# Differential attention: the turn of the last map put ahead of the values on odd steps

## What is computed

```python
sc = jnp.einsum('bqhmd,bkhmd->bhmqk', qblk, k).astype(jnp.float32) + bias
p = jax.nn.softmax(jnp.where(dist >= 0, sc, NEG), axis=-1)
a = p[:, :, 0] - lam * p[:, :, 1]
return jnp.einsum('bhqk,bkhe->bqhe', a.astype(v.dtype), v)
```

## Time and profile before

| | |
|---|---|
| time, median of 3 runs | 1395.96 us (1395.71 to 1396.17) |
| the profiled execution: its time | 1397.49 us |
| the profiled execution: its span | 1395.7 us |
| PE busy in the span | 1341.1 us, 96% |
| DVE, ACT, POOL busy | 47%, 52%, 55% |
| mean granted clock of PE | 0.993 |
| the 32 steps in the span | from 461.3 to 654.4 us |

### The profile page before, as it was taken

The page is one execution under the profiler, slowest core; times in us unless marked ns, Lnnn a source line. Parts: engine busy times, 40 slices in busy tenths (PEclk is TensorE's granted clock), DMA queues, the critical chain, the costliest instruction groups (busy, mean ns, idle before and its releaser), DMA issues.

```text
span 1395.7 us, 20866 instructions
## 1 busy us (share of the span) xinstructions
PE 1341.1 (96%) x7738; PEld 1098.3 (79%) x7738; DVE 652.4 (47%) x1607; ACT 732.5 (52%) x1549; POOL 767.1 (55%) x770
## 2 busy tenths in 40 slices
PE   6999999999999999999999999999999999999997
PEld 4888777777888787877788888778889887778885
DVE  3223068888251455453420011881463347887135
ACT  4244258888343466656433233892534355887252
POOL 5355255677554465665653534687546534586652
PEclk9999998999999999999999999999999999999999
DMA  6232311100434222220443322425226222002322
GB/s 245 97 120 93 121 61 32 31 29 4 163 105 145 101 76 92 76 103 34 156 176 123 111 98 91 152 92 178 93 84 228 100 91 62 1 16 103 139 91 61
DMA packets 28180, 138.65 MB, mean 99 GB/s; under 512 B 3504, under 2 KB 4016, under 8 KB 16688
## 3 DMA queue, kind: packets, MB, share of 16 engines
q1 hardware_dynamic: 14336, 97.52, 19.8%
q10 hardware_dynamic: 13744, 39.79, 8.3%
HBM read 127.86 MB, written 8.39 MB: 98 GB/s over the span
## 4 chain that ended last, share of the span: by engine, by line
PE 76%; DVE 7%; POOL 7%; ACT 6%; issue 2%; DMA 1%; ACTq 0%; POOLq 0%; SPq 0%; DVEq 0%
PE psum L463 51%; PE psum L497 10%; DVE w_free L1453 2%; PE psum L1400 2%; POOL w_free L1572 2%; PE psum L1353 2%; PE psum L1381 2%; PE psum L1022 2%; ACT w_free L908 2%; POOL w_lo L418 2%; PE psum L996 2%; DVE u_lo L1466 1%; ACT u_hi L1511 1%; PE psum L1366 1%; POOL split L1589 1%
## 5 line engine op out<-in xcount | busy, mean ns | idle before, releaser
L418 POOL TENSOR_TENSOR w_lo<-w_raw,w_hi 128x512 fp32r<-128x512 f32 (+2 forms) x159 | 426.2, 2696 | 327.1 <-ACT w_hi L409 317.8
L409 ACT ACTIVATE w_hi<-w_raw 128x2048 fp32r<-128x2048 f32 (+1 forms) x91 | 169.0, 1857 | 97.8 <-DMA w_raw<-in_weights 82.5
L463 PE MATMUL psum<-w_hi,split 128*128 128x512 f32 x608 | 195.3, 394 | 3.2 <-POOL w_lo L418 2.2
L463 PE MATMUL psum<-u_lo,w_hi 128*128 128x512 f32 (+1 forms) x492 | 194.1, 395 | 0.0
L463 PE MATMUL psum<-u_hi,w_hi 128*128 128x512 f32 (+1 forms) x492 | 191.7, 390 | 0.0
L463 PE MATMUL psum<-u_hi,w_lo 128*128 128x512 f32 (+1 forms) x492 | 191.7, 390 | 0.0
L908 ACT ACTIVATE w_free<-w_free,neg_max 128x512 f32<-128x512 f32 (+3 forms) x256 | 148.4, 585 | 10.1 <-DVE neg_max L1453 9.1
L1466 DVE TENSOR_TENSOR u_lo<-psum,u_hi 128x512 fp32r<-128x512 f32 (+3 forms) x256 | 124.0, 519 | 30.5 <-ACT u_hi L1511 27.9
L463 PEld LDWEIGHTS psum<-w_hi,split 128*128 128x128 f32 x608 | 114.2, 188 | 27.6 <-POOL w_lo L418 3.1
L463 PE MATMUL psum<-w_hi,u_lo 128*128 128x512 f32 (+2 forms) x352 | 133.9, 381 | 1.6 <-DVE u_lo L868 1.2
L463 PE MATMUL psum<-w_lo,u_hi 128*128 128x512 f32 (+2 forms) x352 | 132.4, 376 | 0.0
(11 more groups left out here) (212 smaller groups left out, 2495.4 us busy)
## 6 DMA issues: line engine op xcount, KB each, us to landing
w_raw<-in_weights SPq DMA_DIRECT2D x88, 1024.0 KB, 4.8
x<-x_scratch ACTq DMA_DIRECT2D x12, 512.0 KB, 5.2
gain<-in_gains ACTq DMA_DIRECT2D x10, 512.0 KB, 5.7
gain<-in_strips ACTq DMA_DIRECT2D x16, 256.0 KB, 2.8
spare<-in_strips ACTq DMA_DIRECT2D x16, 256.0 KB, 2.9
x_scratch<-x ACTq DMA_DIRECT2D x8, 512.0 KB, 4.0
gain<-in_near ACTq DMA_DIRECT2D x8, 512.0 KB, 4.3
w_raw<-in_near ACTq DMA_DIRECT2D x8, 512.0 KB, 3.7
```

The source lines that it names most:

```text
L409: high = nc.scalar.activation(w_hi[b][:, c], w_raw[b][:, c], ACT.Copy)
L418: low = nc.gpsimd.tensor_tensor(w_lo[b][:, c], w_raw[b][:, c], w_hi[b][:, c].bitcast(F32), ALU.subtract)
L463: mm = nc.tensor.matmul(dst, lhs, rhs, start=(a == 0 and k == 0 and (wl, ul) == (0, 1)), stop=(a + 1 == u and k + 1 == nk and (wl, ul) == ...
```

## The change

On odd steps from 3 on, `turn(i - 1)` is issued directly behind `scores(i)`, and `values((i - 3) // 2)` behind it. Even steps, and step 1, which have no values, stay as they are. No instruction is added or taken away, and all waits keep their counts.

```diff
             for i in range(f.steps):
                 scores(i)
+                if i >= 1:
+                    turn(i - 1)
                 if i >= 3 and i % 2 == 1:
                     values((i - 3) // 2)
-                if i >= 1:
-                    turn(i - 1)
                 if i >= 5 and i % 2 == 1:
                     turn_heads((i - 5) // 2)
                 if i < f.steps - 4:
```

## The result

Over 7 runs each, the changed kernel takes 1399.6 us (1398.69 to 1401.94), the kernel before 1395.71 (1393.51 to 1396.73). The ratio is 1.0028, with a 95% interval of 1.0018 to 1.0038: slower by 3.9 us, twice what was forecast. The interval lies above 1, and it reaches to both sides of the 0.2% that the prediction took as the limit of what can be told. The profiled execution took 1399.29, span 1397.4, only 1.7 more than the profiled one of before. Why the two differences disagree is the matter of this case.

What follows compares the result with a forecast made beforehand. PE, busy 50.00 of 50.00 us, was taken to bound the 32 steps. Terms 3.1 - 0.4 - 0.7 = +2.0 us on the median 1395.96 gave 1398.0, range 1395.2 to 1401.0.

Steps and rivals of the forecast that it cites:

- Which turns move ahead of their maps: Odd steps: the turn comes before its combined map is done in 3 of 15 swaps, steps 9, 17 and 25.
- The tight ones: Steps 3, 29 and 31: maps ready only 0.24, 0.25 and 0.13 us before the turn is due.
- part 5: Steps 10, 18, 26: POOL's earlier pieces may lie beside `combine`; counted 0, with 0.1 to 0.3 us each if it runs over.
- The rival of more waits: Steps 3, 11, 19, 27, 29 and 31 run over by 0.1 us each: +2.5 us in all; chance 0.07.
- part 1: Steps 9, 17, 25: PE waits 1.03 us each, 3.1 in all, from 1.74 shortened by earlier exponentials and POOL pieces.
- In its strict form: Shared-port lock as full block: `combine(8)` needs its whole 0.35 us behind POOL's end, 0.2 more per wait; +2.6, chance 0.06.
- part 2: Step 31: PE's one wait for the last combined map goes, 0.4 us gained, bounds 0.26 and 0.7.
- part 3: PE in 15 odd steps: a cheaper seam from transpose to value product, 0.05 us each, 0.7 gained.
- part 4: Odd steps: values move 0.1 to 0.4 us later; costs nothing, as head squares come after the exponentials; nothing gained.
- The sum: Whole kernel: 3.1 for waits, less 0.4 for the last turn and 0.7 for seams, gives +2.0 us.
- one fall on top of the forecast: Clock rival: behind the three waits PE's granted clock falls once, costing 1.7 us: +3.7, 1399.7 us; chance 0.14.
- the clock falls behind them: Sign that the prediction is wrong: the granted clock falls behind the waits of steps 9, 17 and 25.

Runs made afterwards that it cites:

- the second set of runs: The changed kernel itself measured once more against the kernel before, with a second trace: 1400.86 us (5 runs), ratio 1.0037.
- the two runs that move POOL's pieces: Against the changed kernel: units of steps 7, 15, 23 split one step later (1393.92 us), or only POOL's second two pieces of each one step later (1394.18 us).
- two chunks ahead: Against the changed kernel: in steps 9, 17 and 25 two chunks of fill (six products) between scores and turn; 1395.23 us, ratio 0.9994.
- the run without the three steps: Against the changed kernel: steps 9, 17 and 25 back to the old order, twelve swaps stay; 1394.61 us, ratio 0.9996.

## Why the prediction was right, and where it fell short

- **Which turns move ahead of their maps.** Three of 15, in steps 9, 17 and 25, as forecast. The tight ones held: in steps 3, 29 and 31 PE lost nothing. `combine(10)` did fall beside POOL's pieces (1.61 us in the trace of the changed kernel), as part 5 feared, and so did `combine(18)` and `combine(26)`. They ended 0.4, 0.2 and 0.4 ahead of their turns, where the kernel before had over 1.5 to spare. The rival of more waits, which gave them 0.1 to 0.3, was near.
- **The size of the wait (part 1).** Forecast 1.03, measured 1.02 (0.97 by the step, which holds the seam too, and 0.95 in the list of waits). Both halves of the argument were tested: without the other twelve swaps, that of step 7 among them, the wait is 1.7, and without POOL's pieces there is none. The lock rule of the Trainium skill (SBUF — State Buffer, "SBUF: two separate sides") agrees with that: with POOL's pieces moved, both slow instructions of DVE take their own time. That the lock is the reason was not tested apart. In its strict form it would have made the wait 0.2 longer. The row was nearer: `combine(8)` ended 0.14 behind POOL's pieces again (512.39 against 512.25).
- **The last turn (part 2).** 0.4 forecast, 0.44 measured, and step 31 alone gives it.
- **The seams (part 3).** 0.7 forecast, with 0.05 for each of 15. Measured: 0.05 with 21 value products, but only 0.02 with nine (0.05 in step 3, where no heads are turned behind), together 0.4 in the eleven steps from 3 to 29 without a wait. The seams of the other four steps are inside the 0.97 and the 0.44.
- **The values later (part 4).** Nothing for PE, as forecast, even with six products more ahead of them. The reason was not quite as given: in seven steps ACT's head squares do wait for the values, 6.7 us in all, and it is ACT's idle time that pays.
- **The sum.** These terms give 3 x 0.97 - 0.44 - 0.4 = +2.1, against a forecast of +2.0. The measured difference is 3.9, and 5.6 in the second set of runs. What fell short is the term for the clock, which the sum has at nothing. The prediction names the falls as a rival, one fall on top of the forecast, +3.7 and 1399.7, with a chance of 0.14, and by its own sign ("the clock falls behind them") it is wrong on this point. The first measurement, 1399.6, lies on that rival's time, but not for its reason: the traces show two falls each, not one. With 4 falls behind 6 waits, and 1.6 each, three waits bring 3.2 on the average. +2.1 and +3.2 is 5.3, between the two measured differences, at the upper end of the first interval (2.5 to 5.3) and inside the second (3.5 to 6.8). The reason given for the low chance was that a wait of 1.0 is shorter than the 1.60 which stayed without a fall. The second trace shows why this was no evidence: the same wait goes both ways.
- **Smaller slips.** The rival of more waits adds 0.1 in each of six steps, which is +2.6, not +2.5.

So the waits, the steps and the gains came as forecast, and the cost of the clock did not. That the range held the time is in part luck: three falls in most executions would have given about +6.9, 1402.9, above the range.

What stays open is why a given wait has a fall behind it in one execution and not in the next. The wait is needed in these steps: where the new order stands there and the map is there in time, the clock stays full (0 of 6 in the two runs that move POOL's pieces, 0 of 3 with two chunks ahead). In steps 9, 17 and 25 falls were more frequent with longer waits: 0 of 3 at 0.3 us, 4 of 6 at 1.0, 3 of 3 at 1.7 with about twice the cost. But length alone does not decide. Ahead of step 0 PE waits 1.5 us in all ten traces, and a fall follows in three (the kernel before, the run without the three steps, the run with step 31 only). In the output projection behind the stage it waits 1.6 to 2.1 us in all ten (the idle of 674 to 678 in the earlier trace rows), and the clock never falls. These are few cases.

## What to carry to other kernels

On an engine that is never idle, the order of two pieces matters only through what each waits for. Put the piece whose input is surely there first, for it is the cover of the other. A wait on PE costs more than its length where the clock can fall behind it, so price it as the wait plus the chance of a fall, and do not take one gap without a fall as a sign that the next has none. And when a piece is late, look at who lies beside it on another engine: two POOL instructions moved by one step took the wait away and kept all that the new order gains.

## What the runs showed that was not expected

- Three waits of 1.7 us (5.0 in all) made the kernel 14 us slower: each was followed by a long stretch at a low granted clock (behind the first 0.62 over 8 us, 0.90 over the 4 ahead), 3.2 us lost for each.
- The lowest time is that of the new order with the split one step later, 0.9987 (0.9978 to 0.9996) of the kernel before, and the only one here that its interval calls faster. It is not shown to be better than moving POOL's second pieces alone: the intervals overlap, and the stage takes 190.46 and 190.47 us. In its trace, steps 9, 17 and 25 take 7.46 us instead of the 10.1 or 8.5 of the changed one.
